# mLSTM rows of two layers spread in one fp32r pass, and the squares of a head summed on VectorE ahead of one ones product

## The reference, cut to what matters

```python
li = (p['ml_i'] + ml_b_i); lf = jax.nn.log_sigmoid(p['ml_f'] + ml_b_f)
hm = mlstm_chunkwise(heads(mq, 4), heads(mk, 4), heads(p['ml_v'], 4), li, lf)
hm = hm * jax.nn.sigmoid(heads(p['ml_o'], 4))
y_ml = rmsnorm(hm, ml_norm_g.reshape(4, 256)).reshape(b, s, 1024) * jax.nn.silu(p['ml_z'])
```

## Time and profile before

| what | value |
|---|---|
| runs, median (ends) | 2341.04 us (2339.58 to 2342.08) |
| span of the profiled execution | 2341.0 us; the page gives no other time for this execution |
| TensorE (PE) busy | 2245.5 us, 96% of the span |
| VectorE (DVE) busy | 1193.9 us, 51% |
| ScalarE (ACT) busy | 947.8 us, 40% |
| GpSimd (POOL) busy | 898.2 us, 38% |
| mean granted TensorE clock | 0.992 of full speed |

### The profile page before, as it was taken

The page is one execution under the profiler, slowest core; times in us unless marked ns, Lnnn a source line. Parts: engine busy times, 40 slices in busy tenths (PEclk is TensorE's granted clock), DMA queues, the critical chain, the costliest instruction groups (busy, mean ns, idle before and its releaser), DMA issues. The chain is left out here.

```text
span 2341.0 us, 38427 instructions
## 1 busy us (share of the span) xinstructions
PE 2245.5 (96%) x16046; PEld 1743.2 (74%) x16046; DVE 1193.9 (51%) x2014; ACT 947.8 (40%) x1364; POOL 898.2 (38%) x678
## 2 busy tenths in 40 slices
PE   7999999999999999999999988878999999999997
PEld 5776777787877857777788777776666778888885
DVE  5544834334245467342343878854644657317334
ACT  5423355345353324654343433324266342222243
POOL 4342343334434404333344422222333445545543
PEclk9999999999999999999999989999999999999998
DMA  4221221222222202222233200002211232232332
GB/s 159 84 85 36 73 90 64 72 73 85 98 81 81 90 22 87 81 66 79 68 106 104 72 3 4 4 19 77 72 64 57 81 105 91 99 99 91 99 99 72
DMA packets 50568, 175.18 MB, mean 75 GB/s; under 512 B 6036, under 2 KB 7004, under 8 KB 50396
## 3 DMA queue, kind: packets, MB, share of 16 engines
q1 hardware_dynamic: 50396, 172.73, 22.5%
HBM read 170.60 MB, written 2.11 MB: 74 GB/s over the span
## 5 line engine op out<-in xcount | busy, mean ns | idle before, releaser
L349 POOL TENSOR_TENSOR w_low<-work,w_high 128x512 fp32r<-128x512 f32 x622 | 835.6, 1365 | 1245.2 <-ACT w_high L298 1245.2
L279 PE MATMUL ps<-x_high_tiles,w_high 128*128 128x512 f32 x1544 | 624.9, 405 | 17.5 <-POOL w_low L349 10.9
L298 ACT ACTIVATE w_high<-work 128x1024 fp32r<-128x1024 f32 x311 | 329.2, 1059 | 733.7 <-PE ps L279 730.3
L279 PE MATMUL ps<-x_low_tiles,w_high 128*128 128x512 f32 x1544 | 604.0, 391 | 0.8 <-DVE x_low_tiles L371 0.8
L279 PE MATMUL ps<-x_high_tiles,w_low 128*128 128x512 f32 x1544 | 603.5, 391 | 0.0
L279 PE MATMUL ps<-arena_parts,w_high 128*128 128x512 f32 x1264 | 397.6, 391 | 4.3 <-DVE arena L437 1.6
L279 PEld LDWEIGHTS ps<-x_high_tiles,w_high 128*128 128x128 f32 x1544 | 291.0, 188 | 118.4 <-issue 44.5
L279 PEld LDWEIGHTS ps<-x_low_tiles,w_high 128*128 128x128 f32 x1544 | 290.9, 188 | 64.2 <-DVE x_low_tiles L371 1.6
L279 PEld LDWEIGHTS ps<-x_high_tiles,w_low 128*128 128x128 f32 x1544 | 291.4, 189 | 63.3 <-issue 6.0
L279 PEld LDWEIGHTS ps<-arena_parts,w_high 128*128 128x128 f32 x1264 | 237.3, 188 | 56.8 <-issue 3.2
L279 PE MATMUL ps<-arena_parts,w_low 128*128 128x512 f32 x608 | 236.6, 389 | 0.0
(11 more groups left out here) (452 smaller groups left out, 2864.5 us busy)
## 6 DMA issues: line engine op xcount, KB each, us to landing
work<-w_first SPq DMA_DIRECT2D x178, 512.0 KB, 3.7
work<-w_second SPq DMA_DIRECT2D x134, 512.0 KB, 3.6
xT_sb<-xT SPq DMA_DIRECT2D x8, 256.0 KB, 6.0
outT<-arena SPq DMA_DIRECT2D x8, 256.0 KB, 2.1
arena<-distance_bias SPq DMA_DIRECT2D x4, 256.0 KB
small<-small SPq DMA_DIRECT2D x1, 815.5 KB, 4.5
arena<-consts SPq DMA_DIRECT2D x1, 544.0 KB, 3.8
base<-consts SPq DMA_DIRECT2D x1, 512.0 KB
```

Of the source, the lines that this page charges most:

```text
L279: ins = pe.matmul(out, lhsT, rhs, start=(n == 0 and k == 0 and q == 0), stop=(n == unit["granules"] - 1 and k == len(ops[i]) - 1 and q == 2))
L298: act.activation(m.wh[:, split_of(g), :], m.raw[:, raw_of(g), :], ACT.Copy).then_inc(sem["high_ready"], 1)
L349: pool.tensor_tensor(m.wl[:, split_of(g), part], m.raw[:, raw_of(g), part], m.wh[:, split_of(g), part].bitcast(F32), ALU.subtract).then_in ...
```

## The change

Two tiles are added, `row_parts` and `pick_parts`, 36 partitions x 512 in fp32r, set to zero by GpSimd at the start. `pick_parts` gets `pick` at partitions 0 to 3 and again at 32 to 35 (two ScalarE copies). To spread a row tile, ScalarE copies it to partitions 0 to 3 (the high part), VectorE writes the row less that part to partitions 32 to 35 (the low part), and one fp32r matmul per head over the 36 partitions takes the place of the float32 one. For the norm's sums, VectorE adds the two squared tiles and one float32 ones product per head remains; TensorE's part of `mlstm_norm` is moved two turns later (41, 45, 49, 53; 57, 59, 61, 63), VectorE's adds stand in turns 19, 21, 23, 25, and its reads of the spreads in turns 29 to 32.

```diff
+        for at in (0, ROW_LOW):
+            act.activation(m.pick_parts[at:at + ML_H, :], m.pick[0:ML_H, :], ACT.Copy)
...
+ROW_LOW, ROW_PARTS = 32, 32 + ML_H
+def row_high(act, m, row):
+    return act.activation(m.row_parts[0:ML_H, :], row, ACT.Copy)
+def row_low(dve, m, row):
+    return dve.tensor_tensor(m.row_parts[ROW_LOW:ROW_PARTS, :], row, m.row_parts[0:ML_H, :].bitcast(F32), ALU.subtract)
+def spread_row(pe, m, out, h):
+    return pe.matmul(out, m.pick_parts[:, h * P:(h + 1) * P], m.row_parts, start=True, stop=True)
...
-            pe.matmul(m.ps[:, rbank[h % 2], :], m.pick[0:ML_H, h * P:(h + 1) * P], G, start=True, stop=True).then_inc(sem["ml_rows_ready"], 1)
+            spread_row(pe, m, m.ps[:, rbank[h % 2], :], h).then_inc(sem["ml_rows_ready"], 1)
...
-        yield from turns(2 * start + 3)
+        yield from turns(2 * start + 5)
         for h in range(ML_H):
-            for e in range(2):
-                pe.wait_ge(sem["ml_sq"], 2 * h + e + 1)
-                ins = pe.matmul(m.ps[0:ML_H, bank, :], m.one_column[:, 3 - h:7 - h], m.ml_squares[:, e, :],
-                                start=(h + e == 0), stop=(h + e == ML_H))
-            ins.then_inc(sem["ml_sum"], 1)
+            pe.wait_ge(sem["ml_pair"], h + 1)
+            pe.matmul(m.ps[0:ML_H, bank, :], m.one_column[:, 3 - h:7 - h], m.ml_squares[:, 0, :],
+                      start=(h == 0), stop=(h == ML_H - 1)).then_inc(sem["ml_sum"], 1)
             yield from turns(4)
         for h in range(ML_H):
-            pe.wait_ge(sem["ml_rstd"], 1)
+            pe.wait_ge(sem["ml_low"], 1)
             if h:
                 pe.wait_ge(sem["ml_spread_read"], h)
-            pe.matmul(m.ps[:, bank, :], m.pick[0:ML_H, h * P:(h + 1) * P], rstd, start=True, stop=True).then_inc(sem["ml_spread"], 1)
+            spread_row(pe, m, m.ps[:, bank, :], h).then_inc(sem["ml_spread"], 1)
...
     def vector(dve, sem):
-        yield from turns(start + 2 * ML_H)
+        yield from turns(start + 1)
+        for h in range(ML_H):
+            dve.wait_ge(sem["ml_sq"], 2 * h + 2)
+            dve.tensor_tensor(m.ml_squares[:, 0, :], m.ml_squares[:, 0, :], m.ml_squares[:, 1, :], ALU.add).then_inc(sem["ml_pair"], 1)
+            yield from turns(2 if h < ML_H - 1 else 1)
         dve.wait_ge(sem["den_ready"], 1)
         dve.wait_ge(sem["ml_sum"], ML_H)
...
+        yield
+        dve.wait_ge(sem["ml_high"], 1)
+        row_low(dve, m, rstd).then_inc(sem["ml_low"], 1)
         yield from turns(2)
```

More of the change, by code:

```diff
@@ L926, in vector @@
         yield from turns(3)
+        dve.wait_ge(sem["g_high"], 1)
+        row_low(dve, m, G).then_inc(sem["g_low"], 1)
         dve.wait_ge(sem["u_turned"], 1)
@@ L940, in scalar @@
         own.op(act.activation(em, em, ACT.Exp, scale=-1.0))
+        row_high(act, m, G).then_inc(sem["g_high"], 1)
         yield from turns(2)
@@ L956, in tensor @@
         last.then_inc(sem["u_turned"], 1)
-    return Side(["gates_dve", "gates_act", "z_ready", "log_ready", "u_ready", "u_turned"], tensor, scalar, vector)
+    return Side(["gates_dve", "gates_act", "z_ready", "log_ready", "u_ready", "u_turned", "g_high", "g_low"], tensor, scalar, vector)
 def mlstm_last(m, bank, start):
@@ L1020, in tensor @@
         pe.wait_ge(sem["relu_ready"], (T - 1) * IDX_H)
+        pe.wait_ge(sem["g_low"], 1)
         head_rows(0)
@@ L1147, in scalar @@
         act.activation(rstd, rstd, ACT.Exp, scale=-0.5).then_inc(sem["ml_rstd"], 1)
+        act.wait_ge(sem["ml_rstd"], 1)
+        row_high(act, m, rstd).then_inc(sem["ml_high"], 1)
     def vector(dve, sem):
-        yield from turns(start + 2 * ML_H)
+        yield from turns(start + 1)
[3 more added lines that the diff above has]
+            yield from turns(2 if h < ML_H - 1 else 1)
         dve.wait_ge(sem["den_ready"], 1)
@@ L1163, in vector @@
         dve.wait_ge(sem["ml_spread_read"], ML_H)
-    return Side(["ml_sq", "ml_sum", "ml_total", "ml_log", "ml_rstd", "ml_spread", "ml_spread_read"], tensor, scalar, vector)
+    return Side(["ml_sq", "ml_pair", "ml_sum", "ml_total", "ml_log", "ml_rstd", "ml_high", "ml_low", "ml_spread", "ml_spread_read"], tensor, scalar, vector)
 def gla_side(m, banks, qkv_jobs, act_jobs):
@@ L2590, in build @@
         scal = sb("scal", [P, 4])
+        m.row_parts, m.pick_parts = (ctx.enter_context(nc.sbuf_tensor(name, [P, S], F32R))[0:ROW_PARTS, :] for name in ("row_parts", "pick_parts"))
         m.eps, m.gn_eps, m.sub_eps, m.ten_ln2 = (scal[:, n:n + 1] for n in range(4))
@@ L2775, in build @@
         scalars = [(m.eps, EPS), (m.gn_eps, 64e-5), (m.sub_eps, 1e-5), (m.ten_ln2, 10 * math.log(2.0))]
+        scalars += [(parts.bitcast(F32), 0.0) for parts in (m.row_parts, m.pick_parts)]
         scalars += [(m.one_column[:, n:n + 1], float(n == 3)) for n in range(7)]
```

## The result

The change is slower by 0.36%: 2349.06 us (median of six runs, 2345.89 to 2353.32) against 2341.49 us (six runs of the kernel before, 2338.87 to 2342.36), ratio 1.0036 with a 95% interval of 1.0026 to 1.0046. The forecast was 2337.8 us with 2331.5 to 2344.5; it missed by 11.3 us.

A forecast was written before the change was run, and what follows sets the result against it. The prediction took TensorE's instruction stream to bound the norm's stage: 2341.0 us less 21.2 us of removed matmuls plus 18.0 us of new waits gives 2337.8 us, with a range of 2331.5 to 2344.5 us.

The forecast's parts named there:

- What bounds the kernel: Layer one's norm stretch: TensorE busy for all 110.00 us, so what leaves its stream is gained unless it then waits.
- The removed matmuls: Two layers: rows of G gain 6.6 us, spreads of rstd 7.4, ones products 7.2; together 21.2 us, bounds 19.0 to 26.2.
- my lower bound: Gain per spread, G or rstd: the old spread's own step less 0.31 us for the new one, 0.74 us each.
- The waits: TensorE waits 2.7, 1.3, 2.7 us at heads 0 to 2, 2.3 us ahead of the last spread; 18.0 us, two layers.
- the dearer case: VectorE's adds of heads 0 to 2 all meet GpSimd: 0.45 us more at heads 0 and 2, sum 1.8 us worse.
- What costs nothing: ScalarE's copies into `pick_parts`, GpSimd's zeroing, and high and low parts fit idle time or come early enough; no cost.
- The clock: Rival, chance 0.06: TensorE's clock falls in six waits of over 2 us, some 3 us each, giving 2356 us.
- the rival's border of three falls: In the clock rival, falls at 3 us each decide for slower from three on, 2346.8 us against 2345.7.
- the waits don't form: Rival, chance 0.08: VectorE's adds and reads come early enough, TensorE doesn't wait, the whole gain stays: 2319.8 us.

The follow-up runs named there:

- early adds: The change with VectorE's adds one turn earlier and TensorE's sums and spreads back at their old turns: 2325.01 us, ratio 0.9920 to the kernel before.
- float32 spreads: The change with all 16 spreads as float32 matmuls again, adds and waits kept: 2361.16 us, ratio 1.0075 to the kernel before.
- no adds: The change without VectorE's adds, two ones products a head again, the last spread's wait kept: 2338.75 us, ratio 0.9981 to the kernel before.
- earlier read: The change with VectorE reading head 2's factor one turn earlier, ahead of turn 31's output multiply: 2342.27 us, ratio 1.0004 to the kernel before.
- norm ahead: The change with the norm's instructions ahead of the sparse attention's within each turn, on every engine: 2324.57 us, ratio 0.9918 to the kernel before.
- work in the waits: The change with TensorE making matmuls of zero or unread result while it waits: 2342.4 us, ratio 1.0006 to the kernel before.

## Why the prediction was wrong

- **What bounds the kernel: right.** The stretch was TensorE's alone; with the waits gone, what was taken from its stream came off the time (early adds, 2 x (265.50 - 257.33) = 16.3 us by the intervals, 18.1 us by the runs).
- **The removed matmuls: right in kind, too large.** One step that failed is the price of a spread, and it failed in two places. The first is "The nearest row is the first L279 behind float32 transposes, ... I take that": 0.31 us for the new spread. It takes 439.35 - 438.92 = 0.43 us, and 215.92 - 215.49 = 0.43 us in the mLSTM stage. The second is the price of the old one, 1.23 and 1.14 us, read as a stretch with a spread less a stretch without. The spread's own step is 438.38 - 437.32 = 1.06 us, and 217.31 - 216.26 = 1.05 us. The rest belongs to the matmuls ahead of it and stays: transposes take 437.32 - 437.01 = 0.31 us ahead of the old spread and 438.92 - 438.61 = 0.31 us ahead of the new one, not the 0.14 us that they take ahead of a product. So a spread gains about 0.62 us by the rows and 0.60 us by the intervals, where my lower bound was 0.74. That bound rested on the same 0.31 us, so it was no bound on the new matmul from above. Sixteen spreads gave 9.6 us and not 14.0. The ones products gave 6.7 us (2 x 3.37) and not 7.2. Together 16.3 us and not 21.2.
- **The waits: right in place and size.** 17.2 us came of 18.0 forecast. At head 1 the 1.28 us hit my 1.3 us partly by luck: the add took 1.11 us and not the 0.94 us in my sum (1.3 - 0.36), but VectorE reached it only 390.05 - (391.22 - 1.28) = 0.11 us behind TensorE and not 0.36. The adds of heads 0 and 2 took 0.68 us, and GpSimd made low parts only over head 1's. The Trainium skill (GPSIMD Engine Reference, section Specifications) says that GpSimd shares its SBUF interfaces with VectorE and contends with VectorE instructions of two SBUF inputs, as the add is; the 1.11 us agrees, and the dearer case that I derived from it didn't come.
- **What costs nothing: right.** The two copies take 1.26 us and leave 0.33 us of ScalarE's idle 1.53 us; GpSimd still waits 6.97 us ahead of its first low part; and the low part of rstd is done at 435.41, 3.5 us before the spread at 438.92. The first spread of G starts 0.28 us later than before (197.96 against 197.68), but so does the first product, by 0.25 us (10.86 against 10.61).
- **The clock: the step that failed most.** I had it as a rival with a chance of 0.06, so at nothing in the sum, and argued against it: "15.00 - 11.53 = 3.5 us of gaps in 1820 to 1835 left the clock at 1.00, and the new waits lie a granule or more apart in a stage that is otherwise full". Four falls came in the profiled execution all the same; 4 x 1.7 = 6.8 us. The 3.5 us hold one wait of 2.32 us, much like the new ones, and two of 0.7 us. That it passed without a fall in one execution said little: the same wait brings a fall in three of the nine profiles (last section). I also priced a fall at 3 us, from the stretch behind a gap of 6.65 us; it costs 1.7 us, so the rival's border of three falls was wrong too. The Trainium skill (TensorE: Matmul & The Clock Gate, section HAM oscillation) warns that a wait between bursts of matmuls can bring the clock down at every burst; here 13 of the 18 waits of over 2 us in the two hybrid layers of four profiles brought a fall (the change 4 of 6, the float32 spreads 6 of 6, no adds 0 of 2, the earlier read 3 of 4), so the trace agrees mostly, and not for every wait.
- **The sum.** 16.3 us gained, 17.2 us of waits, 6.8 us of falls: 7.7 us slower, and 7.6 us were measured. With the forecast's own prices it was 3.2 us faster. Neither miss alone makes it clearly slower: with the measured waits, the smaller gain alone gives 0.9 us slower and the falls alone 21.2 - 17.2 - 6.8, 2.8 us slower, both under the 4.7 us that tell a change from none. It took both, and the clock was the larger.

That the waits can be had away was a rival too ("the waits don't form", 2319.8 us, a ratio of 0.9909). It names what the early adds did; they reach 0.9920, which the runs alone don't tell from 0.9909, and by the intervals they fall short because the spreads gain less.

## What to carry to other kernels

Where an engine that bounds a stage gets a new producer, look up when the producer comes to it in its own order, and put its work where nothing slow stands ahead of it: another turn for the add, or another place in the same turn, was worth 24 us here by the intervals, from 0.36% slower to 0.80% faster. A wait of some 2 us on a busy TensorE costs more than its length, since the clock may fall behind it; count 1.7 us more for each, more often than not. And price a matmul by its own step in the place where it stands, old and new alike: the nearest row of another shape misled, and so did the difference between a stretch with it and one without.

## What was not expected of the hardware

- The same wait brings a fall in one kernel and none in another: 2.50 us at head 2, none in the change and one with float32 spreads; 2.19 us at the last spread, one in the change and none without adds. Idle time of 0.98 us behind four small spreads brought one in one layer of two, while 1.28 us at head 1 brought none in three profiles. What tells these cases apart wasn't settled.
- It need not be the kernel that differs. The wait of 2.3 us ahead of L2391 in the third block is left as it was by the change and by every experiment. It brought a fall in three of the nine profiles (the norm ahead, the float32 spreads with their waits, work in the waits) and none in the other six, the kernel before among them. The norm ahead, where L2391 is L2422, its timeline of PE and its window:

```profile
1808.49 0.66 PE L2422 MATMUL ps<-base,tmp 128*128 128x128 f32 x4 [2.33 <-DVE tmp L2526]
...
1809.70:1813.00 3.30, 3.30 (x9) 2.57 (x8) 1.80 (x3) 0.09 (x1) 0.00 (x0) 0.50 0.15 57
```

- Four fp32r spreads over 36 partitions in a row take 1.19 us in one group, so an estimated (1.19 - 0.50) / 3 = 0.23 us each, as much as a product over 128 partitions; a single one between transposes and products takes 0.43 us of the stream.
